# Expert weights of a mixture-of-experts layer loaded in runs of 16384 bytes: seven slots of two megabytes, gate and up over all 2048 columns in four banks each

## The chip, the cores and the metric

The kernel runs on one core of one Trainium2 chip. The metric is the device time in microseconds (us) of one execution. The kernel before takes 2652.8 us, the median of three runs (2651.86 to 2654.31).

## The reference, cut to what matters

The program computes two transformer blocks in float32 on 512 tokens of width 1024. The change lies in the last layer alone: 16 experts, each of which takes the 64 tokens that score highest for it.

```
affinity = softmax(h @ w_router + b_router)
gates, idx = top_k(affinity.transpose(0, 2, 1), 64)          # 64 tokens for each of 16 experts
xin = h[idx]
hid = silu(xin @ w_gate[e]) * (xin @ w_up[e])                # w_gate, w_up: 16 x 1024 x 2048
y   = (hid @ w_down[e]) * gates                              # w_down:       16 x 2048 x 1024
out = x + gate2 * zeros.at[idx].add(y)
```

Each of the three weight arrays of an expert is 8.39 MB (8 binary megabytes); all 16 experts together are 402.65 MB, read once.

## The kernel before, in words

The program is written by hand for five engines: SyncE (SP) issues almost all loads, TensorE (PE) multiplies, ScalarE (ACT) and VectorE (DVE) empty the banks of PSUM. Each engine has its own list of instructions in a fixed order and waits on semaphores of the others. Nothing reorders them at run time.

The experts are worked in eight pairs, n = 0 to 7. The two experts of a pair, d = 0 and 1, lie side by side: the 64 tokens of expert d take columns 64d to 64d+63 of the stationary operand and rows 64d to 64d+63 of a bank. For each n the order on PE is (`pe_experts`, L1205 to L1211):

1. `pe_up` (L1121): gate and up. The 2048 hidden columns are taken in two halves of 1024; in a half, gate over eight k, then up over eight k, in two banks of 512 columns each. The transposes of the first half's hidden values (`pe_moe_turn`, 0 and 1) stand between gate and up of the second half.
2. `pe_scatter` of pair n-1 (L1159): eight products that put the last pair's result back to its tokens; DVE adds each of them to the sum (L2396).
3. `pe_gather` of pair n+1 (L1100): the next pair's tokens are picked by products with a 0/1 matrix (L149), which DVE builds in `dve_gather` just before, and are transposed (L587).
4. `pe_down` (L1143): down over 16 k, two banks; the second half's transposes (`pe_moe_turn`, 2 and 3) stand behind k = 3.

The scatter of the last pair ends the program, and then the result is written.

The weights go through a ring of slots (`Ring`, L104): `Ring.load` waits until PE has signalled that it has used the slot's former load, issues the DMA, and the products wait for its landing. In the expert stage the ring has 13 slots of 1 binary megabyte (8192 bytes on each of the 128 partitions): four in RING, four in RB, two each in AT4 and XT, and one in HID3. One load of gate or up is two blocks k of 128 rows and 1024 columns of one expert, and partition p gets row 128k + p: pieces of 4096 bytes, 8192 bytes apart in memory from one partition to the next. One load of down is two consecutive rows for each partition, 8192 bytes in one piece, 32768 bytes apart. PE signals after every two k, and so sets free the two slots (d = 0 and 1) of one step. `sp_experts` (L409) issues the loads in the order of use; SP does nothing else in this stage.

The trace names tiles by a stage's letter: RB_a is RB, AT_g is AT4, HID_e is HID3, CAT_e is the tokens. An fp32 product stands as two records in the trace.

Of the kernel before, what the change touches and what calls it, by code (L numbers as in the profile page):

```python
# [11 lines left out]
NSLOT = 8  # L12
# [144 lines left out]
def build_program(nc, A, K, out):  # L157
    with ExitStack() as ctx:
# [3 lines left out]
        def sem(name):  # L162
            return ctx.enter_context(nc.semaphore(name))
# [8 lines left out]
        XT = sb("XT", [128, 8, 512])  # L172
# [176 lines left out]
        hidden = TMP[:, 0:2, :].rearrange("p a b -> p (a b)")  # L349
# [3 lines left out]
        PTm = [HID3[:, 12288 + 512 * i:12800 + 512 * i] for i in range(2)]  # L353
        xtok = HID3[:, 13312:14336]
# [54 lines left out]
        def sp_experts(sp, w):  # L409
            for n in range(8):  # L410
                for half in range(2):
                    for m, nm in enumerate(("w_gate_2", "w_up_2")):
                        for kp in range(4):
                            for d in range(2):
                                ring.load(sp, w, ("gu", n, half, m, kp, d),
                                          rows_of(A[nm][0, 2 * n + d], 2 * kp, 1024 * half, 2, 1024), (2, 1024),
                                          (T_moe, "gu", n, half, m, kp))
                for kp in range(8):
                    for d in range(2):
                        rows8 = A["w_down_2"][0, 2 * n + d].rearrange("(h p k) n -> h p k n", h=2, k=8)  # L420
                        ring.load(sp, w, ("dn", n, kp, d), rows8[kp // 4, :, 2 * (kp % 4):2 * (kp % 4) + 2, :],
                                  (2, 1024), (T_moe, "dn", n, kp))

        def sync_program(sp):
# [35 lines left out]
            ring.many, ring.i = NSLOT + 5, 0  # L460
            for i in range(4, 8):
                ring.freed[i] = ((T_out, "out2", 1, 3),)
            for i in range(2):
                ring.freed[NSLOT + i] = ((S_moe, "h2", 3, 1), (T_moe, "router"))
                ring.freed[NSLOT + 2 + i] = ((S_moe, "acc", 3, 1),)
            ring.freed[NSLOT + 4] = ((T_moe, "pos"),)
# [649 lines left out]
        def pe_moe_turn(pe, w, n, fg):  # L1116
            b = banks.take(w, ("hid", n, fg), (S_moe, "hid", n, fg))
            w.wait_ge(*V_moe.at("act", n, fg | 1))
            transposes(pe, b, [hidden[:, 4 * (fg % 2) + j::8] for j in range(4)]).then_inc(*T_moe.up("hid", n, fg))

        def pe_up(pe, w, n):  # L1121
            xv_ = xins[n % 2]
            w.wait_ge(*V_moe.at("xt", n, 0))
            w.wait_ge(*S_moe.at("xt", n, 1))
            for half in range(2):
                fgs = (2 * half, 2 * half + 1)
                for m in range(2):
                    bs = [banks.take(w, ("up" if m else "gate", n, fg), *(((V_moe, "act", n, fg),) if m else
                                                                         ((S_moe, "silu", n, fg),))) for fg in fgs]
                    for k in range(8):  # L1130
                        for c, b in enumerate(bs):
                            for d in range(2):
                                w.wait_ge(*ring.landed("gu", n, half, m, k // 2, d))
                                wv = ring.view("gu", n, half, m, k // 2, d)[:, k % 2, 512 * c:512 * (c + 1)]
                                last = pe.matmul(b[64 * d:64 * d + 64, :], xv_[:, k, 64 * d:64 * d + 64], wv,  # L1135
                                                 start=k == 0, stop=k == 7)
                        if k % 2:
                            last.then_inc(*T_moe.up("gu", n, half, m, k // 2))
                    if half and m == 0:
                        pe_moe_turn(pe, w, n, 0)  # L1140
                        pe_moe_turn(pe, w, n, 1)

        def pe_down(pe, w, n):  # L1143
            bs = [banks.take(w, ("down", n, hf), (V_moe, "y", n, hf)) for hf in range(2)]
            for k in range(16):
                w.wait_ge(*S_moe.at("hid", n, k // 4))
                for hf, b in enumerate(bs):
                    for d in range(2):
                        w.wait_ge(*ring.landed("dn", n, k // 2, d))
                        wv = ring.view("dn", n, k // 2, d)[:, k % 2, 512 * hf:512 * (hf + 1)]  # L1150
                        last = pe.matmul(b[64 * d:64 * d + 64, :], hidT[:, k, 64 * d:64 * d + 64], wv,  # L1151
                                         start=k == 0, stop=k == 15)
                if k % 2:
# [511 lines left out]
        def act_gather(act, w, n):  # L1665
            x = n % 2
            w.wait_ge(*T_moe.at("x", n, 1))
            if n:
                w.wait_ge(*T_moe.at("xt", n - 1, 1))
            act.activation(xtok[:, 512:1024], banks.of("x", n, 1), ACT.Copy, bias=0.0, scale=1.0).then_inc(  # L1670
                *S_moe.up("x", n, 1))
            w.wait_ge(*T_moe.at("pt", n))
            if n >= 2:
                w.wait_ge(*T_moe.at("sc", n - 2, 3, 1))
            act.activation(PTm[x], banks.of("pt", n), ACT.Copy, bias=0.0, scale=1.0).then_inc(*S_moe.up("pt", n))
            w.wait_ge(*T_moe.at("xt", n, 1))
            if n >= 2:
                w.wait_ge(*T_moe.at("gu", n - 2, 1, 1, 3))
            act.activation(xins[x][:, 4:8, :], banks.of("xt", n, 1).rearrange("p (k n) -> p k n", n=128), ACT.Copy,
                           bias=0.0, scale=1.0).then_inc(*S_moe.up("xt", n, 1))  # L1680

        def act_moe_hidden(act, w, n, fg):
            w.wait_ge(*T_moe.at("hid", n, fg))
            if n:
                w.wait_ge(*T_moe.at("dn", n - 1, 7))
# [3 lines left out]
        def act_experts(act, w):  # L1689
# [22 lines left out]
            for n in range(8):  # L1712
                for fg in range(4):
                    q = act_tmp.seat(w, fg % 2, ("hid", n, fg), (T_moe, "hid", n, fg | 1))
                    w.wait_ge(*T_moe.at("gu", n, fg // 2, 0, 3))
                    if fg > 1:
                        act_moe_hidden(act, w, n, fg - 2)
# [4 lines left out]
                act_moe_hidden(act, w, n, 2)  # L1722
                act_moe_hidden(act, w, n, 3)
# [645 lines left out]
        def dve_gather(dve, w, n):  # L2369
# [3 lines left out]
            for i in range(4):  # L2373
                for d in range(2):
# [4 lines left out]
                                      ALU.mult).then_inc(*V_moe.up("P", n, i, d))  # L2379
            w.wait_ge(*T_moe.at("x", n, 0))  # L2380
# [4 lines left out]
            if n >= 2:  # L2385
                w.wait_ge(*T_moe.at("gu", n - 2, 1, 1, 3))
# [11 lines left out]
        def dve_experts(dve, w):  # L2398
# [32 lines left out]
            w.wait_ge(*V_moe.at("pos"))  # L2431
            dve_gather(dve, w, 0)
            for n in range(8):
                for fg in range(4):
                    q = act_tmp.of("hid", n, fg)
                    w.wait_ge(*S_moe.at("silu", n, fg))
                    w.wait_ge(*T_moe.at("gu", n, fg // 2, 1, 3))
# [6 lines left out]
                w.wait_ge(*T_moe.at("dn", n, 7))  # L2444
# [37 lines left out]
        for t in (banks, act_tmp, dve_tmp, lg_tmp, pads, PTs, ring):  # L2482
            t.restart()
# [116 lines left out]
```

## Time and profile before

| | |
|---|---|
| median of 3 runs | 2652.8 us |
| the profiled execution | 2654.73 us |
| its span | 2652.9 us |
| PE busy | 2366.4 us (89%) |
| DVE busy | 1031.9 us (39%) |
| ACT busy | 621.8 us (23%) |
| DMA, mean over the span | 224 GB/s |
| mean granted TensorE clock | 0.958 of 2.4 GHz |

The span is the profiled execution from its first to its last instruction. A share of a busy engine is an average over stages with different limits: the expert stage is the last 40% of the span, and the rows below are mostly from it. DMA share is the mean busy share of the core's 16 DMA engines; packets that overlap make it a little more than 1.

### The profile page before, as it was taken

What the parts mean: (1) busy time and instruction counts of PE and PEld (TensorE: products, weight loads), DVE (VectorE), ACT (ScalarE), POOL (GpSimd) and SP (SyncE); (2) the same over time, 40 slices, a digit from 0 to 9 for tenths busy, and PEclk for the clock granted to TensorE, in tenths of its full rate; (3) what the DMA queues carried; (4) which work ended last, traced back from release to release, by engine and by line L of the source; (5) the groups of instructions that cost most, each with busy time, mean ns of one, the idle gap of its engine ahead of it and who ended that gap; (6) DMA issues with size and microseconds to landing.
All of it is one profiled execution on the core that took longest, in us unless ns stands there. A gap on an engine that the chain in (4) does not pass through costs nothing.

```text
span 2652.9 us, 23645 instructions
## 1 busy us (share of the span) xinstructions
PE 2366.4 (89%) x9809; PEld 1390.5 (52%) x9809; DVE 1031.9 (39%) x1633; ACT 621.8 (23%) x1000; POOL 129.2 (5%) x133
## 2 busy tenths in 40 slices
PE   5999988899999599999789888887989797988888
PEld 2446444688887288888667647332323233332323
DVE  4565462566654866564656353110101101010102
ACT  2112162323322333223446454000000000000000
POOL 2000000000000200000321322000000000000000
PEclk8999988999999699999889998899999999999999
DMA  8312410255552145550211203799999999999998
GB/s 344 103 64 87 147 68 25 104 191 183 179 190 88 55 149 184 190 190 18 93 56 32 76 29 128 301 423 419 397 421 401 421 400 422 398 409 413 407 418 333
DMA packets 181440, 594.21 MB, mean 224 GB/s; under 512 B 12418, under 2 KB 13952, under 8 KB 163798
## 3 DMA queue, kind: packets, MB, share of 16 engines
q1 hardware_dynamic: 177938, 583.24, 57.1%
q0 software_dynamic: 3088, 9.33, 1.0%
q8 instruction: 77, 1.26, 0.2%
q14 instruction: 29, 0.24, 0.0%
q10 hardware_dynamic: 308, 0.13, 0.0%
HBM read 590.54 MB, written 2.13 MB: 223 GB/s over the span
## 4 chain that ended last, share of the span: by engine, by line
PE 69%; DMA 18%; DVE 8%; ACT 3%; issue 1%; SPq 1%; POOL 0%; ACTq 0%; DVEq 0%; POOLq 0%
PE PS L863 9%; PE PS L865 9%; PE PS L864 9%; PE PS L679 7%; PE PS L1151 7%; PE PS L889 5%; PE PS L149 5%; PE PS L1135 5%; DMA RING<-in_w_up_dram 3%; DMA RB_a<-in_w_up_dram 3%; PE PS L1165 2%; DMA RING<-in_w_gate_dram 2%; DMA XT<-in_w_up_dram 2%; PE PS L587 2%; PE PS L763 2%; DMA XT<-in_w_gate_dram 1%
## 5 line engine op out<-in xcount | busy, mean ns | idle before, releaser
L2438 DVE TENSOR_TENSOR TMP<-TMP,PS 128x512 f32<-128x512 f32 x32 | 20.6, 684 | 559.1 <-PE PS L1135 559.1
L1135 PE MATMUL PS<-RING,HID_e 128*64 128x512 f32 x656 | 186.3, 597 | 33.5 <-DMA RING<-in_w_up_dram 18.9
L1135 PE MATMUL PS<-RB_a,HID_e 128*64 128x512 f32 x624 | 178.2, 597 | 27.9 <-DMA RB_a<-in_w_up_dram 16.5
L1135 PEld LDWEIGHTS PS<-RING,HID_e 128*64 128x64 f32 x656 | 57.9, 136 | 133.1 <-issue 69.4
L1135 PE MATMUL PS<-XT,HID_e 128*64 128x512 f32 x320 | 110.2, 597 | 15.6 <-DMA XT<-in_w_up_dram 8.6
L1135 PEld LDWEIGHTS PS<-RB_a,HID_e 128*64 128x64 f32 x624 | 56.9, 137 | 118.1 <-issue 62.7
L1135 PE MATMUL PS<-AT_g,HID_e 128*64 128x512 f32 x296 | 102.4, 597 | 13.0 <-DMA AT_g<-in_w_up_dram 7.7
L1686 ACT ACTIVATE HID_e<-PS 128x512 f32<-128x512 f32 x32 | 18.3, 598 | 386.2 <-PE PS L587 386.2
L863 PE MATMUL PS<-AH_b,WH_b 128*128 128x512 f32 x256 | 101.8, 398 | 3.2 <-DVE AL_b L1805 3.2
L863 PE MATMUL PS<-AH_d,WH_d 128*128 128x512 f32 x256 | 101.8, 398 | 3.2 <-DVE AL_d L1805 3.2
L865 PE MATMUL PS<-AH_b,WL_b 128*128 128x512 f32 x256 | 100.6, 393 | 0.0
L865 PE MATMUL PS<-AH_d,WL_d 128*128 128x512 f32 x256 | 100.6, 393 | 0.0
L864 PE MATMUL PS<-AL_b,WH_b 128*128 128x512 f32 x256 | 100.5, 393 | 0.0
L864 PE MATMUL PS<-AL_d,WH_d 128*128 128x512 f32 x256 | 100.5, 393 | 0.0
L2448 DVE TENSOR_TENSOR HID_e<-PS,HID_e 128x512 f32<-128x512 f32 x16 | 10.3, 686 | 231.9 <-PE PS L1151 231.9
L863 PE MATMUL PS<-HH_d,WH_d 128*128 128x512 f32 x256 | 100.4, 392 | 0.0
L863 PE MATMUL PS<-HH_b,WH_b 128*128 128x512 f32 x256 | 100.4, 392 | 0.0
L865 PE MATMUL PS<-HH_b,WL_b 128*128 128x512 f32 x256 | 99.9, 390 | 0.0
L865 PE MATMUL PS<-HH_d,WL_d 128*128 128x512 f32 x256 | 99.9, 390 | 0.0
L864 PE MATMUL PS<-HL_b,WH_b 128*128 128x512 f32 x256 | 99.7, 390 | 0.0
L864 PE MATMUL PS<-HL_d,WH_d 128*128 128x512 f32 x256 | 99.7, 390 | 0.0
L149 PE MATMUL PS<-CAT_e,HID_e 128*128 128x512 f32 x128 | 71.2, 721 | 31.3 <-DVE HID_e L2378 31.3
(447 smaller groups left out, 4591.6 us busy)
## 6 DMA issues: line engine op xcount, KB each, us to landing
RB_a<-in_w_gate_dram SPq DMA_DIRECT2D x42, 1024.0 KB, 16.6
RING<-in_w_gate_dram SPq DMA_DIRECT2D x41, 1024.0 KB, 17.8
RING<-in_w_up_dram SPq DMA_DIRECT2D x41, 1024.0 KB, 18.1
RB_a<-in_w_down_dram SPq DMA_DIRECT2D x41, 1024.0 KB, 21.1
RING<-in_w_down_dram SPq DMA_DIRECT2D x38, 1024.0 KB, 23.6
RB_a<-in_w_up_dram SPq DMA_DIRECT2D x36, 1024.0 KB, 18.0
RING<-in_mlp_w_dram SPq DMA_DIRECT2D x32, 1024.0 KB, 5.7
RB_a<-in_mlp_w_dram SPq DMA_DIRECT2D x32, 1024.0 KB, 5.4
```

What stands on the lines that cost most here:

```text
L149: last = pe.matmul(out, l, r, start=i == 0, stop=i == len(pairs) - 1)
L587: last = pe.transpose(out[0:n, 128 * i:128 * i + x.shape[0]], x, ident[0:x.shape[0], 0:x.shape[0]])
L679: last = pe.matmul(b, ring.view(name, *label, k // 4)[:, k % 4, j * 128:(j + 1) * 128], rhs(k), start=k == 0, stop=k == 7)
L763: last = pe.matmul(b, lhs, ring.view("v", k // 4)[:, k % 4, :], start=False, stop=k == 7)
L863: pe.matmul(b, hi[:, kk, js], a[:, k, :], start=k == 0, stop=False)
L864: pe.matmul(b, hi[:, kk, js], al[:, k, :], start=False, stop=False)
L865: last = pe.matmul(b, lo[:, kk, js], a[:, k, :], start=False, stop=k == 7)
L889: last = pe.matmul(b, x, y, start=k == 0 and i == 0, stop=k == 7 and i == 2)
L1135: last = pe.matmul(b[64 * d:64 * d + 64, :], xv_[:, k, 64 * d:64 * d + 64], wv, start=k == 0, stop=k == 7)
L1151: last = pe.matmul(b[64 * d:64 * d + 64, :], hidT[:, k, 64 * d:64 * d + 64], wv, start=k == 0, stop=k == 15)
L1165: pe.matmul(b, PTm[n % 2][:, i * 128:(i + 1) * 128], yB[:, hf * 512:(hf + 1) * 512], start=True, stop=True).then_inc(*T_moe.up("sc", n, i, ...
L2438: dve.tensor_tensor(q, q, banks.of("up", n, fg), ALU.mult).then_inc(*V_moe.up("act", n, fg))
```

## The change

The ring of 13 slots of 1 binary megabyte in the expert stage becomes a ring `big` of seven slots of 2: RING in two, RB in two, AT4, XT, and HID3 from column 12288 (it was one slot from 14336). Two small buffers, `xtok` and `PTm`, move out of HID3 into PADS for that.

Gate and up are loaded so that partition p gets eight consecutive rows, 8p to 8p+7, over all 2048 columns; one load is two of them, 16384 bytes in one piece, 65536 bytes apart from one partition to the next. One load of down is four consecutive rows, 16384 bytes, 32768 bytes apart. There are 24 loads for a pair in place of 48. The tokens are transposed with a stride of 8 columns to match.

PE goes over gate in four banks, all eight k, and then over up in four banks. All four transposes of hidden values stand at the head of `pe_down`. A gate or up step now uses two loads of 2 binary megabytes and signals after two k; a step of down signals after four k in place of two. The hidden values take four TMP buffers in place of two. On DVE the building of the 0/1 matrices for pair n+1 (`dve_chosen`) moves from behind the scatter of n-1 to ahead of the products of gate and up of n. The first transpose of the gathered tokens now waits for both halves of `xtok`, where each waited for its own.

```diff
-        hidden = TMP[:, 0:2, :].rearrange("p a b -> p (a b)")
+        hid_tmp = Turns([TMP[:, i, :] for i in range(4)])
+        hidden = TMP[:, 0:4, :].rearrange("p a b -> p (a b)")
+        loose = PADS[:, :, :].rearrange("p a b -> p (a b)")
...
-        for i, ap in enumerate([AT4[:, 0:4, :], AT4[:, 4:8, :], XT[:, 0:4, :], XT[:, 4:8, :]]):
-            ring.add(ap.rearrange("p a b -> p (a b)"), sem(f"ring{NSLOT + i}"))
-        ring.add(HID3[:, 14336:16384], sem(f"ring{NSLOT + 4}"))
+        big = Ring()
+        for i, ap in enumerate([RING[:, 0:2, :], RING[:, 2:4, :], RB[:, 0:2, :], RB[:, 2:4, :], AT4[:, :, :], XT[:, :, :]]):
+            big.add(ap.rearrange("p a b -> p (a b)"), sem(f"big{i}"))
+        big.add(HID3[:, 12288:16384], sem("big6"))
...
         def sp_experts(sp, w):
             for n in range(8):
-                for half in range(2):
-                    for m, nm in enumerate(("w_gate_2", "w_up_2")):
-                        for kp in range(4):
-                            for d in range(2):
-                                ring.load(sp, w, ("gu", n, half, m, kp, d),
-                                          rows_of(A[nm][0, 2 * n + d], 2 * kp, 1024 * half, 2, 1024), (2, 1024),
-                                          (T_moe, "gu", n, half, m, kp))
-                for kp in range(8):
+                for m in range(2):
+                    for kp in range(4):
+                        for d in range(2):
+                            rows8 = A[("w_gate_2", "w_up_2")[m]][0, 2 * n + d].rearrange("(p k) n -> p k n", k=8)
+                            big.load(sp, w, ("gu", n, m, kp, d), rows8[:, 2 * kp:2 * kp + 2, :], (2, 2048),
+                                     (T_moe, "gu", n, m, kp))
+                for kq in range(4):
                     for d in range(2):
                         rows8 = A["w_down_2"][0, 2 * n + d].rearrange("(h p k) n -> h p k n", h=2, k=8)
-                        ring.load(sp, w, ("dn", n, kp, d), rows8[kp // 4, :, 2 * (kp % 4):2 * (kp % 4) + 2, :],
-                                  (2, 1024), (T_moe, "dn", n, kp))
+                        big.load(sp, w, ("dn", n, kq, d), rows8[kq // 2, :, 4 * (kq % 2):4 * (kq % 2) + 4, :], (4, 1024),
+                                 (T_moe, "dn", n, kq))
...
-                w.wait_ge(*(S_moe if hf else V_moe).at("x", n, hf))
-                transposes(pe, b, [xtok[:, (4 * hf + k) * 128:(4 * hf + k + 1) * 128] for k in range(4)]).then_inc(
+                w.wait_ge(*V_moe.at("x", n, 0))
+                w.wait_ge(*S_moe.at("x", n, 1))
+                transposes(pe, b, [xtok[:, 4 * hf + k::8] for k in range(4)]).then_inc(
...
         def pe_down(pe, w, n):
+            for t in range(4):
+                pe_moe_turn(pe, w, n, t)
             bs = [banks.take(w, ("down", n, hf), (V_moe, "y", n, hf)) for hf in range(2)]
...
-                if k % 2:
-                    last.then_inc(*T_moe.up("dn", n, k // 2))
-                if k == 3:
-                    pe_moe_turn(pe, w, n, 2)
-                    pe_moe_turn(pe, w, n, 3)
+                if k % 4 == 3:
+                    last.then_inc(*T_moe.up("dn", n, k // 4))
...
             for n in range(8):
+                if n < 7:
+                    dve_chosen(dve, w, n + 1)
                 for fg in range(4):
-                    q = act_tmp.of("hid", n, fg)
+                    q = hid_tmp.of("hid", n, fg)
```

## Rows read from the trace of the kernel before

**Rows 1.** The page: the span, what DMA moved in 40 equal slices, and packets.

```profile
span 2652.9 us, 23645 instructions
GB/s 344 103 64 87 147 68 25 104 191 183 179 190 88 55 149 184 190 190 18 93 56 32 76 29 128 301 423 419 397 421 401 421 400 422 398 409 413 407 418 333
DMA packets 181440, 594.21 MB, mean 224 GB/s; under 512 B 12418, under 2 KB 13952, under 8 KB 163798
```

**Rows 2.** Windows, stretches of one pair: length, engines' busy time, PEclk, DMA share, GB/s.

```profile
1885.00:1892.00 7.00, 7.00 (x38) 2.81 (x37) 0.69 (x1) 1.41 (x3) 0.00 (x0) 1.00 0.63 236
1900.00:1907.00 7.00, 7.00 (x35) 2.31 (x33) 0.00 (x0) 0.00 (x0) 0.00 (x0) 1.00 1.01 369
1907.00:1983.00 76.00, 64.31 (x288) 22.26 (x284) 2.58 (x4) 3.15 (x6) 0.00 (x0) 1.00 1.03 419
```

**Rows 3.** Windows: down alone (first, last of six pairs), gate and up alone (likewise).

```profile
1865.00:1885.00 20.00, 16.14 (x37) 6.99 (x38) 10.46 (x27) 0.28 (x1) 0.00 (x0) 0.91 1.01 428
2479.00:2499.00 20.00, 16.13 (x38) 6.98 (x38) 10.40 (x27) 0.38 (x1) 0.00 (x0) 0.91 1.01 426
...
1930.00:1982.00 52.00, 40.66 (x180) 14.56 (x178) 1.29 (x2) 2.07 (x4) 0.00 (x0) 1.00 1.03 421
2544.00:2596.00 52.00, 40.31 (x179) 14.02 (x176) 1.29 (x2) 2.06 (x4) 0.00 (x0) 1.00 1.03 419
```

**Rows 4.** The chain that ended last, one turnover: start us, us, what.

```profile
1843.05 18.19 DMA RING<-in_w_up_dram
...
1861.28 3.65 PE PS L1135 x14
1864.93 7.08 PE PS L1165 x16
...
1875.86 8.83 PE PS L149 x16
1884.69 1.34 PE PS L587 x12
1886.03 7.02 PE PS L1151 x32
1893.05 1.09 PE PS L587 x8
```

**Rows 5.** Windows of 1 us in the dip; the last two columns are DMA share and GB/s.

```profile
1885.00:1886.00 1.00, 1.00 (x12) 0.78 (x9) 0.40 (x1) 0.81 (x2) 0.00 (x0) 1.00 0.89 377
...
1887.00:1888.00 1.00, 1.00 (x8) 0.30 (x6) 0.00 (x0) 0.00 (x0) 0.00 (x0) 1.00 0.50 213
...
1890.00:1891.00 1.00, 1.00 (x8) 0.31 (x6) 0.00 (x0) 0.00 (x0) 0.00 (x0) 1.00 0.87 197
```

**Rows 6.** Timeline of SP's DMA issues, two turnover rows and the first after the start.

```profile
1864.97 25.49 SPq L132 DMA_DIRECT2D RING<-in_w_down_dram  x4
1893.09 0.33 SPq L132 DMA_DIRECT2D RB_a<-in_w_down_dram  x1
...
1685.26 3.80 SPq L132 DMA_DIRECT2D RING<-in_w_up_dram  x3
```

**Rows 7.** Timeline of PE: start, us, what, and in brackets the idle time before.

```profile
1861.28 3.65 PE L1135 MATMUL PS<-RING,HID_e 128*64 128x512 f32 x14 [1.43 <-DMA RING<-in_w_up_dram]
...
1875.86 8.83 PE L149 MATMUL PS<-CAT_e,HID_e 128*128 128x512 f32 x16 [3.86 <-DVE HID_e L2378]
...
488.83 1.02 PE L628 MATMUL PS<-ones,TMP 128*128 128x1 f32 x8 [2.98 <-DVE MODC L1769]
```

**Rows 8.** Windows behind those idle times: the third number from the end is the granted clock.

```profile
1876.00:1880.00 4.00, 4.00 (x6) 1.69 (x7) 0.00 (x0) 0.00 (x0) 0.00 (x0) 0.57 1.01 428
1880.00:1884.00 4.00, 4.00 (x10) 1.72 (x9) 0.69 (x1) 0.00 (x0) 0.00 (x0) 1.00 1.01 426
...
490.50:496.00 5.50, 2.29 (x9) 2.02 (x10) 2.41 (x4) 2.68 (x4) 0.00 (x0) 0.50 1.05 400
```

**Rows 9.** Windows at the start of the stage, DMA's last two columns.

```profile
1672.00:1685.00 13.00, 12.27 (x42) 5.58 (x43) 1.38 (x2) 2.97 (x4) 0.00 (x0) 0.89 0.02 6
```

**Rows 10.** The chain that ended last, the last pair.

```profile
2602.12 7.06 PE PS L1165 x16
...
2637.62 3.66 PE PS L1151 x14
```

More of the change, by code:

```diff
@@ L352, in build_program @@
         Pg = [HID3[:, 11264 + 512 * i:11776 + 512 * i].rearrange("p (t n) -> p t n", t=4) for i in range(2)]
[L353 to L357 removed]
+        PTm = [loose[:, 1024 + 512 * i:1536 + 512 * i] for i in range(2)]
+        xtok = loose[:, 0:1024]
+        big = Ring()
+        for i, ap in enumerate([RING[:, 0:2, :], RING[:, 2:4, :], RB[:, 0:2, :], RB[:, 2:4, :], AT4[:, :, :], XT[:, :, :]]):
+            big.add(ap.rearrange("p a b -> p (a b)"), sem(f"big{i}"))
+        big.add(HID3[:, 12288:16384], sem("big6"))
         parts = [(T_ml, "xm"), (T_ml, "so"), (T_ml, "av"), (T_dil, "ak"), (T_dil, "aq"), (T_out, "out2", 0),
@@ L459, in sync_program @@
                     ring.load(sp, w, (*parts[b][1:], kh), rows_of(W, 4 * kh, c0), (4, 512), (G_prt, b, 4 * kh + 3))
[L460 to L466, printed above, removed]
+            big.many = 7
+            big.freed[0] = (*ring.freed[0], *ring.freed[1])
+            big.freed[1] = (*ring.freed[2], *ring.freed[3])
+            big.freed[2] = big.freed[3] = ((T_out, "out2", 1, 3),)
+            big.freed[4] = ((S_moe, "h2", 3, 1), (T_moe, "router"))
+            big.freed[5] = ((S_moe, "acc", 3, 1),)
+            big.freed[6] = ((T_moe, "pos"),)
             sp_experts(sp, w)
@@ L1111, in pe_gather, with pe_moe_turn @@
                 b = banks.take(w, ("xt", n, hf), (S_moe if hf else V_moe, "xt", n, hf))
-                w.wait_ge(*(S_moe if hf else V_moe).at("x", n, hf))
-                transposes(pe, b, [xtok[:, (4 * hf + k) * 128:(4 * hf + k + 1) * 128] for k in range(4)]).then_inc(
+                w.wait_ge(*V_moe.at("x", n, 0))
+                w.wait_ge(*S_moe.at("x", n, 1))
+                transposes(pe, b, [xtok[:, 4 * hf + k::8] for k in range(4)]).then_inc(
                     *T_moe.up("xt", n, hf))
[L1116 to L1119, printed above, removed]
+        def pe_moe_turn(pe, w, n, t):
+            b = banks.take(w, ("hid", n, t), (S_moe, "hid", n, t))
+            w.wait_ge(*V_moe.at("act", n, t | 1))
+            o = 1024 * (t // 2) + 4 * (t % 2)
+            transposes(pe, b, [hidden[:, o + j:1024 * (t // 2 + 1):8] for j in range(4)]).then_inc(*T_moe.up("hid", n, t))
         def pe_up(pe, w, n):
@@ L1124, in pe_up @@
             w.wait_ge(*S_moe.at("xt", n, 1))
[L1125 to L1136, printed above, removed]
-                        if k % 2:
[L1138 to L1141, printed above, removed]
+            for m in range(2):
+                bs = [banks.take(w, ("up", n, fg), (V_moe, "act", n, fg)) if m else
+                      banks.take(w, ("gate", n, fg), (S_moe, "silu", n, fg)) for fg in range(4)]
+                for k in range(8):
+                    for c, b in enumerate(bs):
+                        for d in range(2):
+                            w.wait_ge(*big.landed("gu", n, m, k // 2, d))
+                            wv = big.view("gu", n, m, k // 2, d)[:, k % 2, 512 * c:512 * (c + 1)]
+                            last = pe.matmul(b[64 * d:64 * d + 64, :], xv_[:, k, 64 * d:64 * d + 64], wv,
+                                             start=k == 0, stop=k == 7)
+                    if k % 2:
+                        last.then_inc(*T_moe.up("gu", n, m, k // 2))
         def pe_down(pe, w, n):
+            for t in range(4):
+                pe_moe_turn(pe, w, n, t)
             bs = [banks.take(w, ("down", n, hf), (V_moe, "y", n, hf)) for hf in range(2)]
@@ L1148, in pe_down @@
                     for d in range(2):
-                        w.wait_ge(*ring.landed("dn", n, k // 2, d))
-                        wv = ring.view("dn", n, k // 2, d)[:, k % 2, 512 * hf:512 * (hf + 1)]
+                        w.wait_ge(*big.landed("dn", n, k // 4, d))
+                        wv = big.view("dn", n, k // 4, d)[:, k % 4, 512 * hf:512 * (hf + 1)]
                         last = pe.matmul(b[64 * d:64 * d + 64, :], hidT[:, k, 64 * d:64 * d + 64], wv,
                                          start=k == 0, stop=k == 15)
-                if k % 2:
-                    last.then_inc(*T_moe.up("dn", n, k // 2))
-                if k == 3:
-                    pe_moe_turn(pe, w, n, 2)
-                    pe_moe_turn(pe, w, n, 3)
+                if k % 4 == 3:
+                    last.then_inc(*T_moe.up("dn", n, k // 4))
         def pe_scatter(pe, w, n):
@@ L1721, in act_experts @@
                     act_gather(act, w, n + 1)
-                act_moe_hidden(act, w, n, 2)
-                act_moe_hidden(act, w, n, 3)
+                for t in range(4):
+                    act_moe_hidden(act, w, n, t)
         def scalar_program(act):
@@ L2379, in dve_gather @@
                                       ALU.mult).then_inc(*V_moe.up("P", n, i, d))
+        def dve_gather(dve, w, n):
+            x = n % 2
             w.wait_ge(*T_moe.at("x", n, 0))
@@ L2481, in build_program @@
             s.restart()
-        for t in (banks, act_tmp, dve_tmp, lg_tmp, pads, PTs, ring):
+        for t in (banks, act_tmp, dve_tmp, lg_tmp, hid_tmp, pads, PTs, ring, big):
             t.restart()
```

19 lines of the change are left out of this document (9 added, 10 removed).

## The prediction

> **What bounds the kernel now.** I read the page's slices first. DMA moves about 400 to 420 GB/s from slice 27 to 39 [rows 1]: the expert stage streams its 402.65 MB near one constant rate, so I then took one pair of experts apart. From the scatter at 1864.93 to the last pair's at 2602.12 there are six pairs in 737.2 us, 122.87 us each [rows 4, 10]. In that time 50.33 MB must come. Windows over stretches with one kind of load give the rates: gate and up, in 4096-byte packets, 421 to 419 GB/s, down, in 8192-byte packets, 428 to 426, with DMA share 1.01 to 1.03 in both [rows 3]. So 33.55 MB / 0.420 = 79.9 us and 16.78 / 0.4265 = 39.3 us. Two flaws are left. In 1885 to 1892 the rate is 236, which loses 7 x (1 - 236/426.5) = 3.1 us; in 1900 to 1907 it is 369 at full share, which loses 0.85 us [rows 2]. Sum 123.2 us, 0.3 more than the measured period. The DMA engines are the bound, and the dip is the only time in which they lack work.
>
> The dip's cause stands in the chain and the timeline of SP. Call T the landing of a pair's last up load (1861.28) and E the end of its products (1864.93). From E on PE scatters (7.08 us), waits 3.86 us for DVE, gathers (8.83), transposes (1.34), and only the first two k of down (half of the 7.02 us for four) set slots free: 1889.5, T + 28.25 [rows 4, 7]. SP's row of four loads that starts at 1864.97 ends at 1890.46: two went out at E, two after that release [rows 6]. Meanwhile the 13 slots hold 13.63 MB, 32.0 us of transfer at 426.5. At 1887 the share is exactly 0.50 with 213 GB/s [rows 5]: half of the DMA engines have drained, the others are some 4 us behind, and work resumes around 1890.5.
>
> **The change part by part.**
>
> *Packet size.* A 4096-byte packet on one of 16 engines takes 4096 x 16 / 420 GB/s = 156.0 ns, one of 8192 bytes 307.3 ns [rows 3]. The line through both is 4.7 ns plus 151.3 ns for 4096 bytes; an estimate for 16384 bytes from it is 609.9 ns, 430 GB/s. No such packet of a load is in the trace. Bounds: the 8192-byte rate of 426.5 from below if larger packets bring nothing more, 433 from above with no cost per packet (8192 x 16 / 302.6); rows for a worse end are weighed as a rival. I take 430, since share and rate speak for engines that are bound by themselves. Per pair: gate and up 78.0 us (-1.9), down 39.0 (-0.3): -2.2 us.
>
> The Trainium skill (DMA: Bandwidth & Descriptors, section Why small descriptors are slow (HBM only)) says that each packet costs about three cycles of the engine's internal bus beside its beats of 32 bytes. An estimate by that page would be 515 cycles for 16384 bytes, 433 GB/s with its 850 MHz, and a pair 0.7 us shorter than in my sum; the trace's 4.7 ns lies above its 3.5.
>
> *Fewer issues.* 24 loads in place of 48. SP's issues wait for room or for slots and are never what the chain waits for at the turnover except through the slot; gain 0, bounds 0 and 0.33 us (one issue [rows 6]) per turnover.
>
> *Coarser steps at T.* A step of gate or up was 16 records in two 1 MB loads and is 32 in two 2 MB loads. Of the old step 14 records ran after the last landing, 3.65 us [rows 4]; of the new one 30, that is 3.65 + 3.45 = 7.1 us. E comes 3.45 us later against T, each pair.
>
> *The chain from E to the first release.* Scatter 7.08 as before; DVE has four products to do at E where it had two, but PE's fifth scatter needs their banks only after 3.5 us, four times 0.69. The wait of 3.86 us goes, since the 0/1 matrices are built during gate; with it goes the low clock behind it: granted 0.57 in the next 4 us, 1.00 after [rows 8], that is between the 1.2 and 2.4 GHz levels, so the gather at full clock takes 16 x 0.43 = 6.9 us, not 8.83. The transposes of tokens now wait for ACT's copy of the second half, some 0.5 us, and take a strided operand as those of the hidden values do, 1.09 / 8 = 0.136 us against 1.34 / 12 = 0.112 [rows 4]: 2.0 us in place of 1.34. All four hidden transposes stand ahead of down: 16 x 0.136 = 2.2 us. The first release comes after four k, 7.02 us. Sum 7.08 + 6.9 + 2.0 + 2.2 + 7.0 = 25.2 us, against 24.6 before. ACT's three copies and the first hidden copy, 0.6 us each, end inside PE's transposes. With the coarser step the release moves from T + 28.25 to T + 32.3: +4.05.
>
> *The ring's depth.* Seven slots hold 14.68 MB, 34.1 us at 430: +2.1 against 32.0. So the dip grows by 4.05 - 2.1 = 1.9 us, from 3.1 to 5.0. What waits behind this release on SP is the whole next stream, and through it PE.
>
> *Clock in gate and up.* PE now works 6.9 us and idles about 2.7 of every 9.75, where it idled 1.43 of 5 at granted clock 1.00 [rows 2, 7]. An idle time of 2.98 us was followed by 0.50 [rows 7, 8]. A fall during the last step of a pair makes E up to 1.7 us later (as much as the gather loses now: 8.83 - 6.9 = 1.9). Elsewhere DMA hides it: 6.9 + 1.9 < 9.75. Bounds 0 and 1.9; I take 0.5, nearer to the rows with 1.00.
>
> *A pair with a dip:* -2.2 + 1.9 + 0.5 = +0.2 us, six times: +1.2.
> *Pair 0 to 1:* no scatter, so release at T + 25.2 and no dip; -2.2.
> *The start:* DMA stands still from 1672 with all slots full until PE's first release near 1685.2 [rows 6, 9]. That release comes 3.45 us (coarser step) and 0.6 us (transposes) later, but 1.05 MB more has landed: of pair 0's gate and up 18.87 MB are left at 430 (43.9 us) in place of 19.92 at 420 (47.4): +0.55.
> *The end:* the last down is bound by its landings; transfer -0.3, and 30 records follow the last landing in place of 14: +3.45 - 0.3 = +3.15 [rows 10].
> The moves of buffers, the order of banks, the four TMP buffers: 0, as each is freed by work many microseconds back; bounds 0 and 0.6 (one ACT copy) per pair.
>
> Sum: 1.2 - 2.2 + 0.55 + 3.15 = +2.7 us, on the profiled execution's 2654.73 us (span 2652.9 [rows 1]). That execution lies 1.9 us above the median of the runs, and the forecast is made on the median: 2655.5.
>
> **Rivals.**
>
> *The dip doesn't grow (faster).* If the two halves of the DMA engines drain together, or the chain is shorter than summed, the gain of the packets is kept: 7 x -2.2 + 0.55 + 3.15 = -11.7, 2641; with the dip gone as well (-3.1 x 6) 2622. For it: the lag of half the engines is what opens the dip early [rows 5], and the slow stretch of 369 GB/s [rows 2] may be where it arises; both may change. Against: the release itself comes 4 us later.
>
> *The turnover decides (slower).* Place: PE between T and the first release of down. With the low clock in the last step (+1.9 in place of 0.5) and no gain beyond the 8192-byte rate (-1.2 for gate and up), a pair is -1.2 + 1.9 + 1.9 = +2.6: 6 x 2.6 - 1.2 + 0.8 + 3.4 = +18.6, 2671. It decides from the point where dip and clock together grow by more than the 2.2 us that packets give. For it: the rows on 2.98 us of idle time; against: 1.43 us never cost anything.
>
> *The change doesn't do what it says.* Packets might be cut to 8192 bytes: then only gate and up gain 1.2 us, a pair with a dip is +1.2, and the sum 7.2 - 1.2 + 0.8 + 3.4 = +10, 2663. For it: no load in the trace has larger ones; against: the packets below 8 KB leave 17642 others [rows 1], as many as down's 16384 pieces need, so pieces go out whole so far.
>
> *Distance in memory.* Gate and up come from addresses 65536 bytes apart per partition, where it was 8192. If that made every gate and up load as slow as the stretch of 369 GB/s, 33.55 MB would take 90.9 us, +11 a pair and some +90 in all; a tenth of that is +9, 2662. Against: down at 32768 is the faster one [rows 3].
> The Trainium skill (DMA: Bandwidth & Descriptors, Latency and other measured facts, HBM row pitch) reports loss at row pitches of large powers of two, small at 512 KiB (207 GB/s against 214) and large from 2 MiB; by it 64 KiB would cost at most those 3%, which no run here shows.
>
> **How the numbers follow.** Forecast 0.38; dip no larger 0.25; turnover decides 0.20; packets cut 0.10; distance 0.07. A difference under 0.2% (5.3 us) can't be told from none here. The forecast case is mostly within it (0.30 same, 0.05 slower, 0.03 faster), the second faster (0.23, 0.02 same), the third slower (0.17, 0.03 same), the fourth too (0.09, 0.01), the fifth slower (0.07): faster 0.26, same 0.36, slower 0.38. The forecast's own range is 2648 to 2662; with the rivals' ends 2636 to 2673.
>
> **What would show it.** Rate over gate and up near 430 in place of 420, and half as many DMA issues, show the packets. The dip should last about 2 us longer and begin about 2 us later after T; no idle time of PE ahead of the gather and a gather of 6.9 us show the moved DVE work; idle times of 2.7 us with granted clock 1.00 or not show the clock. At the end 30 records follow the last landing. Wrong would be: a period under 120 us (dip not grown), a rate at or under 420 (packets or distance), or a chain from E to the first release far from 25 us.

## The result and the profile after

The changed kernel takes 2626.56 us (median of 4 runs, 2625.84 to 2627.95) against 2653.14 us for the kernel before beside it: ratio 0.9901, 95% interval 0.9883 to 0.9918. That is 26.6 us faster; the forecast was 2.3 us slower, with a range down to 2636. It was wrong.

The page after, with the lines that answer to [rows 1] (the last one is the queue of SP's loads):

```profile
span 2626.1 us, 23460 instructions
GB/s 348 104 65 80 136 89 4 109 192 192 192 189 84 64 144 179 190 186 39 88 49 33 92 29 129 212 431 431 424 430 410 430 422 431 412 416 426 415 430 326
DMA packets 121024, 594.19 MB, mean 226 GB/s; under 512 B 9346, under 2 KB 10881, under 8 KB 95191
q1 hardware_dynamic: 117522, 583.23, 56.1%
```

The slices of the expert stage rise from about 400 to 420 to 410 to 431, and 60,416 packets fewer move the same bytes, so the loads did go out in larger pieces. (By size, 402.65 MB in pieces of 16384 bytes need 24,576 packets, and 81,920 in pieces of 4096 and 8192: 57,344 fewer. The other 3,072 are packets under 512 bytes, 16 for each of the 192 loads that are gone.)

The windows of the changed kernel over down alone (first and last of six pairs) and over gate and up alone, which answer to [rows 3]; the last three columns are the granted clock, DMA share and GB/s:

```profile
1859.00:1879.00 20.00, 19.66 (x71) 10.03 (x72) 8.84 (x14) 3.64 (x7) 0.00 (x0) 1.00 1.01 431
2458.00:2478.00 20.00, 19.66 (x74) 9.92 (x74) 8.37 (x14) 3.64 (x7) 0.00 (x0) 1.00 1.01 429
...
1922.00:1974.00 52.00, 39.69 (x168) 12.23 (x166) 0.00 (x0) 2.06 (x4) 0.00 (x0) 0.93 1.01 430
2530.00:2582.00 52.00, 43.12 (x170) 14.01 (x167) 4.99 (x9) 2.06 (x4) 0.00 (x0) 0.93 1.01 431
```

Both kinds now run at 429 to 431, where the line through the two rates of before gave 430. The granted clock is 0.93 in the gate and up windows, where it was 1.00.

The chain of waits of the changed kernel over one turnover, the last step of two more and the end, which answers to [rows 4, 10]:

```profile
1852.18 7.08 PE PS L1137 x30
1859.26 7.07 PE PS L1163 x16
1866.33 6.88 PE PS L149 x16
1873.97 2.90 PE PS L589 x24
1876.88 27.62 PE PS L1152 x128
...
2208.84 8.78 PE PS L1137 x30
...
2568.43 8.47 PE PS L1137 x30
...
2607.43 7.09 PE PS L1152 x30
```

Each step is there as it was summed: 30 records behind the landing in 7.08 us, no wait ahead of the gather, a gather of 6.88 us, and the transposes, which with the wait ahead of them take 3.7 us from the gather's end to down where 4.2 were forecast. In the other two turnovers the last step takes 8.78 and 8.47 us. Over the six turnovers behind pairs 1 to 6 it took 7.08 us twice and 8.5 to 8.8 us four times. There the clock was low. The idle time of PE ahead of such a step, and the granted clock right behind another landing at 1970.93, near the lower of its two levels:

```profile
1852.18 0.64 PE L1137 MATMUL PS<-AT_g,HID_e 128*64 128x512 f32 x1 [2.60 <-DMA AT_g<-in_w_up_dram]
...
1970.50:1974.00 3.50, 3.07 (x8) 1.00 (x10) 0.00 (x0) 0.00 (x0) 0.00 (x0) 0.51 1.01 431
```

SP's issues in the changed kernel in the turnovers that follow 1852.18 and 2208.84; a row's start is the moment of release when SP waited:

```profile
1859.66 0.43 SPq L132 DMA_DIRECT2D AT_g<-in_w_down_dram  x1
1883.93 0.33 SPq L132 DMA_DIRECT2D XT<-in_w_down_dram  x1
...
2218.02 0.43 SPq L132 DMA_DIRECT2D HID_e<-in_w_down_dram  x1
2242.32 0.33 SPq L132 DMA_DIRECT2D RING<-in_w_down_dram  x1
```

Counted from the landing T of the pair's last up load, the first release comes at T + 31.75 (1883.93 - 1852.18) and T + 33.5; the forecast was T + 32.3 and up to 1.9 more. The dip, in windows of the changed kernel: first after the turnover at 1859 (1 row), then 1 us each after the one at 1979, then two of the length that answers to [rows 2] (1900 to 1907 and the rest of the pair):

```profile
1884.00:1886.00 2.00, 2.00 (x12) 0.71 (x10) 0.00 (x0) 0.00 (x0) 0.00 (x0) 1.00 0.83 246
...
2002.00:2003.00 1.00, 1.00 (x6) 0.29 (x4) 0.00 (x0) 0.00 (x0) 0.00 (x0) 1.00 0.35 148
2003.00:2004.00 1.00, 1.00 (x8) 0.34 (x6) 0.00 (x0) 0.00 (x0) 0.00 (x0) 1.00 0.15 66
2004.00:2005.00 1.00, 1.00 (x8) 0.38 (x6) 0.00 (x0) 0.00 (x0) 0.00 (x0) 1.00 0.00 0
2005.00:2006.00 1.00, 1.00 (x6) 0.29 (x4) 0.00 (x0) 0.00 (x0) 0.00 (x0) 1.00 1.15 262
...
1900.00:1907.00 7.00, 7.00 (x36) 2.40 (x34) 2.46 (x9) 0.00 (x0) 0.00 (x0) 1.00 1.02 435
1907.00:1972.00 65.00, 50.28 (x220) 16.07 (x218) 1.91 (x10) 2.06 (x4) 0.00 (x0) 0.96 1.01 430
```

In the kernel before, the row of share 0.50 in [rows 5] stood between two more like it:

```profile
1886.00:1887.00 1.00, 1.00 (x7) 0.43 (x8) 0.29 (x1) 0.60 (x1) 0.00 (x0) 1.00 0.56 238
...
1888.00:1889.00 1.00, 1.00 (x6) 0.29 (x4) 0.00 (x0) 0.00 (x0) 0.00 (x0) 1.00 0.54 229
```

The changed kernel has no such plateau of some 3 us: the engines work at full rate to T + 31 or T + 32 and fall silent nearly together, within 2 us, and the stretch of 369 GB/s [rows 2] is gone (435). From landing to landing a pair takes (2568.43 - 1852.18) / 6 = 119.4 us, before 122.87.

Where the 26.8 us between the two spans lie, by the landings T in the two chains (those of before at 1742.05, 1861.28 and 2598.47; after at 1735.35, 1852.18 and 2568.43): up to pair 0's landing -6.7, of which 1.3 lies ahead of the expert stage; pair 0 to 1 -2.4; the six pairs -20.9; the end +3.2. The stage's first gather, by which I take its start, begins anywhere from 1665.4 to 1671.1 us in the profiled executions of all runs, so a few us of a difference between two spans can lie ahead of anything that was changed. Below, pairs are therefore mostly compared from landing to landing.

### The profile page after: what moved, and what is told of

Read it like the earlier page. It is cut to its first block, busy times and chain, and to the rows that moved or that the text cites. A ratio compares the mean times of both kernels' runs of the same rounds, so it can differ in the third digit from the quotient of the medians.

```text
span 2626.1 us, 23460 instructions
## 1 busy us (share of the span) xinstructions
PE 2361.5 (90%) x9809; PEld 1384.4 (53%) x9809; DVE 1028.1 (39%) x1633; ACT 620.2 (24%) x1000; POOL 129.2 (5%) x133
## 4 chain that ended last, share of the span: by engine, by line
PE 73%; DMA 15%; DVE 7%; ACT 3%; issue 1%; POOL 0%; ACTq 0%; DVEq 0%; POOLq 0%
PE PS L865 9%; PE PS L1137 9%; PE PS L867 9%; PE PS L866 9%; PE PS L681 7%; PE PS L1152 7%; PE PS L891 5%; PE PS L149 5%; DMA RING<-in_w_up_dram 4%; DMA RB_a<-in_w_up_dram 3%; PE PS L1163 2%; PE PS L589 2%; DMA HID_e<-in_w_up_dram 2%; PE PS L765 2%; DMA XT<-in_w_up_dram 2%; DMA AT_g<-in_w_up_dram 2%
## 5 line engine op out<-in xcount | busy, mean ns | idle before, releaser
L1137 PE MATMUL PS<-RING,HID_e 128*64 128x512 f32 x608 | 214.6, 628 | 28.9 <-DMA RING<-in_w_up_dram 20.7
L1137 PE MATMUL PS<-RB_a,HID_e 128*64 128x512 f32 x576 | 202.3, 614 | 28.7 <-DMA RB_a<-in_w_up_dram 21.7
L1137 PE MATMUL PS<-XT,HID_e 128*64 128x512 f32 x288 | 138.5, 633 | 15.7 <-DMA XT<-in_w_up_dram 10.6
L1137 PE MATMUL PS<-HID_e 128*64 128x512 f32 x288 | 136.7, 627 | 17.7 <-DMA HID_e<-in_w_up_dram 11.4
L1137 PE MATMUL PS<-AT_g,HID_e 128*64 128x512 f32 x288 | 136.5, 627 | 11.6 <-DMA AT_g<-in_w_up_dram 7.3
L1137 PEld LDWEIGHTS PS<-RING,HID_e 128*64 128x64 f32 x608 | 64.9, 145 | 125.9 <-issue 83.6
L1714 ACT ACTIVATE TMP<-PS 128x512 f32<-128x512 f32 x32 | 16.5, 603 | 456.9 <-PE PS L1137 456.9
L1137 PEld LDWEIGHTS PS<-RB_a,HID_e 128*64 128x64 f32 x576 | 63.1, 141 | 109.7 <-issue 67.4
```

## The experiments

Every run is compared with the kernel before on the same chip; that one had medians of 2651.5 to 2653.8. "Against the change" is against the 2626.56 us above.

**e1: small packets from the new addresses.** Based on the changed kernel.

Loads of down stay as they are; the issues of gate and up double.

```diff
+    def load_halves(self, sp, w, label, src, *freed):
...
+        view = self.aps[b].rearrange("p (h k c) -> p h k c", h=2, k=2)
+        for h in range(2):
+            sp.dma_start(view[:, h], src[:, :, 1024 * h:1024 * (h + 1)]).then_inc(self.sems[b], 16)
+        self.n[b] += 32
...
-                            big.load(sp, w, ("gu", n, m, kp, d), rows8[:, 2 * kp:2 * kp + 2, :], (2, 2048),
-                                     (T_moe, "gu", n, m, kp))
+                            big.load_halves(sp, w, ("gu", n, m, kp, d), rows8[:, 2 * kp:2 * kp + 2, :],
+                                            (T_moe, "gu", n, m, kp))
```

> The changed kernel, with each gate and up load of two binary megabytes issued as two DMAs of 1024 columns each: packets of 4096 bytes from the same addresses, the same slots and the same steps. Theory A (the lag of half the DMA engines before came from addresses 8192 bytes apart between partitions): no lag, the dip as in the changed kernel, and only the packets' price, 33.55 MB at 420 in place of 431 GB/s = +2.0 us a pair, 7.7 pairs' worth = +16: about 2642 us. Rival B (the lag comes from small packets as such, wherever they come from): the lag and the long dip return as well, +2 to +3 us at each of six turnovers on top: 2655 to 2660 us.

Measured 2642.35 us, ratio 0.9960 (0.9945 to 0.9974). As theory A has it: +15.8 against the change, which is the packets' price alone.

**e2: larger packets from the old addresses.**

```diff
-                            big.load(sp, w, ("gu", n, m, kp, d), rows8[:, 2 * kp:2 * kp + 2, :], (2, 2048),
+                            big.load(sp, w, ("gu", n, m, kp, d),
+                                     rows_of(A[("w_gate_2", "w_up_2")[m]][0, 2 * n + d], 2 * kp, 0, 2, 2048), (2, 2048),
...
```

> The changed kernel, with gate and up loaded as rows 128k + p over all 2048 columns: pieces of 8192 bytes, 8192 bytes apart between partitions, the same slots and steps. Theory A (addresses): the slow stretch after each turnover and the lag of half the engines return, +3 us at six turnovers, beside +1.0 us a pair for packets of 8192 bytes (8 us in all): about 2652 us. Rival B (packet size): only the packets' price and perhaps a little lag: 2634 to 2638 us.

Measured 2631.82 us, ratio 0.9914 (0.9898 to 0.9931). Theory A fails here: rows 8192 bytes apart bring no lag back as long as whole rows are loaded. It is also 2 us below the range of rival B; against the change the packets of 8192 bytes cost 5.3 us where 8 were expected.

**e3: the kernel before with eight rows per partition.**

```diff
-                                          rows_of(A[nm][0, 2 * n + d], 2 * kp, 1024 * half, 2, 1024), (2, 1024),
+                                          A[nm][0, 2 * n + d].rearrange("(p k) n -> p k n", k=8)[
+                                              :, 2 * kp:2 * kp + 2, 1024 * half:1024 * (half + 1)], (2, 1024),
...
```

> The kernel before, with gate and up loaded as eight consecutive rows for each partition (4096-byte pieces, 65536 bytes apart between partitions), tokens transposed to match; 13 slots of one binary megabyte as before. Theory A (addresses): slow stretch and lag go; the slots drain at T + 30 where the release comes at T + 28.3, so the dip of 3.1 us and the slow stretch of 0.85 go six times: -20 to -24, about 2631 us. Rival B (packet size): nothing changes, 2653 us within 3.

Measured 2637.37 us, ratio 0.9937 (0.9923 to 0.9952): -16.5 with packets, slots and steps as before. Rival B fails here. Theory A has the direction right but expected 20 to 24: a pair takes 120.8 us from landing to landing ((2579.37 - 1854.66) / 6), 2.1 less than before and still some 1.8 more than 50.33 MB at its rates. Windows of e3 over its dip and over the stretch that had 369 GB/s, and one of e2 and one of e1 over that stretch:

```profile
1884.00:1888.00 4.00, 4.00 (x23) 1.69 (x19) 0.00 (x0) 0.34 (x1) 0.00 (x0) 1.00 0.92 342
1900.00:1907.00 7.00, 7.00 (x36) 2.37 (x34) 0.00 (x0) 0.00 (x0) 0.00 (x0) 1.00 1.03 421
```

```profile
1900.00:1907.00 7.00, 7.00 (x34) 2.30 (x32) 0.00 (x0) 0.00 (x0) 0.00 (x0) 1.00 1.01 427
```

```profile
1900.00:1907.00 7.00, 7.00 (x34) 2.30 (x32) 0.00 (x0) 0.00 (x0) 0.00 (x0) 1.00 1.02 417
```

In e3 the microseconds of the dip have shares of 0.76, 0.89 and 0.71 (1883 to 1886), so half of the engines no longer run dry 3 us ahead. Neither small packets (e1, e3) nor rows 8192 bytes apart (e2) make the slow stretch or the lag by themselves. It comes with their combination in the kernel before: half a row from each of 128 neighbouring rows. That combination was not tried with the slots and steps of the changed kernel.

The start of the stage says the same. From the first gather to pair 0's landing, across the standstill with full slots, it takes 72.2 us in the kernel before and 71.6 in e4 below, which both have the old loads, and 66.8 in the change, 68.1 in e1, 67.3 in e2 and 67.5 in e3.

**e4: the kernel before with the matrices built early.** This is the DVE part of the change alone.

```diff
             for n in range(8):
+                if n < 7:
+                    dve_chosen(dve, w, n + 1)
                 for fg in range(4):
...
```

> The kernel before, with the 0/1 matrices of pair n+1 built on DVE ahead of the products of pair n, as the change does; nothing else. PE's wait of 3.86 us and the low clock in the gather go, so the first release of down comes 5.8 us earlier, at T + 22.5, before even the first half of the DMA engines has drained (T + 24.6). If all engines bind alike, the whole dip goes: 6 x -3.1 = -18.6, about 2634 us. If the lagging half binds alone (it stood idle only some 1.2 us of each turnover), only that is gained: 6 x -1.2 = -7, about 2646 us. If DMA did not bind at all there, more than -19.

Measured 2631.3 us, ratio 0.9917 (0.9902 to 0.9932): -22.4. The chain of e4: its first turnover and its last landing, then the first gather of the stage in e4 and, last, in the kernel before:

```profile
1856.57 3.65 PE PS L1135 x14
1860.22 7.06 PE PS L1165 x16
1867.29 6.87 PE PS L149 x16
...
1875.50 7.02 PE PS L1151 x32
...
2574.80 3.65 PE PS L1135 x14
...
1665.73 9.60 PE PS L149 x16
...
1669.84 9.59 PE PS L149 x16
```

The wait ahead of the gather and the low clock in it are gone, and the first two k of down end at T + 22.4. Of the 23.0 us between the two spans, 19.0 lie in the six turnovers, 3.2 each, as "the whole dip goes" has it. Another 4.1 lie ahead of the stage, where nothing was changed. A pair takes 119.7 us, 0.5 over the 119.2 of its two rates. Windows of e4 over what were the dip and the slow stretch, and one over its start, behind the standstill with full slots:

```profile
1884.00:1891.00 7.00, 7.00 (x36) 2.42 (x34) 0.00 (x0) 0.28 (x1) 0.00 (x0) 1.00 1.00 422
1891.00:1898.00 7.00, 7.00 (x36) 2.32 (x34) 0.00 (x0) 0.00 (x0) 0.00 (x0) 1.00 1.02 420
...
1695.00:1700.00 5.00, 5.00 (x26) 2.06 (x24) 0.00 (x0) 0.00 (x0) 0.00 (x0) 1.00 1.01 364
```

At the turnover dip and slow stretch are both gone, with the old addresses and packets still in place; at the start, where the standstill stays, so does the slow stretch. So the slow stretch is something that follows a standstill. All engines bind alike. This one part is most of the gain: all the rest of the change adds some 4.7 us to it (2626.56 against 2631.3), and the two intervals overlap.

**e5: the changed kernel with the matrices late again.** The two lines of e4's diff move back behind `dve_scatter`.

> The changed kernel, with the building of the 0/1 matrices put back behind the scatter. PE waits for DVE again (3.9 us) and gathers at the low clock (+1.9), so the first release of down comes 5.8 us later. Theory (DMA engines bind, and stand idle from about T + 32 until that release): the idle time grows by all of it at six turnovers: +35, about 2661 us. If part of the wait lies in slack of PE and the slots still cover it: +10 to +20.

Measured 2664.19 us, ratio 1.0039 (1.0024 to 1.0054): +37.6 against the change. By landings, 31.8 of the 37.3 us between the spans lie in the six turnovers, 5.3 each of the 5.8 expected, and 4.7 between pair 0 and 1, which had no dip in the change. It is 10.4 us slower than the kernel before (2653.84 beside it): without the early matrices, the new loads, slots and steps are a loss. With the wait back, the windows of e5 have 7 us (1889 to 1896) at DMA share 0.12.

```profile
1889.00:1896.00 7.00, 7.00 (x35) 2.30 (x33) 0.00 (x0) 0.13 (x1) 0.00 (x0) 1.00 0.12 49
```

**e6: six slots.**

```diff
-            big.many = 7
+            big.many = 6
```

> The changed kernel with six of its seven slots. 2.1 MB less in flight is 4.9 us of transfer, so the engines drain at T + 27 in place of T + 32: +4.9 us at six turnovers, and +4.9 at the start, where one load less has landed: +34, about 2661 us. If the idle time measured at the turnover were no idle time of the bound (something else ended last there): under +10.

Measured 2657.68 us, ratio 1.0017 (1.0007 to 1.0026): +31.1. By landings a turnover costs 4.0 us more and the start 4.9 more (the profiled execution was the fastest of ten). In the first turnover the engines stand nearly still from 1881 on:

```profile
1881.00:1887.00 6.00, 6.00 (x32) 2.00 (x30) 0.00 (x0) 0.00 (x0) 0.00 (x0) 1.00 0.10 41
```

So the turnover has its price from the side of the supply too, by what the slots hold.

**e7: the same memory in 14 small slots.**

```diff
-                            big.load(sp, w, ("gu", n, m, kp, d), rows8[:, 2 * kp:2 * kp + 2, :], (2, 2048),
-                                     (T_moe, "gu", n, m, kp))
+                            big.load(sp, w, ("gu", n, m, kp, d), rows8[:, kp, :], (2048,), (T_moe, "gu", n, m, kp))
...
-                    if k % 2:
-                        last.then_inc(*T_moe.up("gu", n, m, k // 2))
+                    last.then_inc(*T_moe.up("gu", n, m, k))
...
-            big.many = 7
+            big.many = 14
```

> The changed kernel with the same 14 binary megabytes cut into 14 slots of one: a load of gate or up is one row of 2048 columns per partition, one of down two rows, all in packets of 8192 bytes, and PE signals after each k of gate and up and after two k of down. E comes 3.45 us earlier after T and the first release another 3.5: at about T + 25, before the engines drain, so no dip. A pair is then 50.33 MB at 426.5 GB/s = 118.0 us against 119.6: six times -1.6, pair 0 +1.1, start -3.0, end -3.0: about 2612 us. If packets of 16384 bytes matter more than the steps, slower than 2626.

Measured 2619.59 us, ratio 0.9868 (0.9853 to 0.9883). Faster than the change, by 7 in place of the 14 expected; the two intervals just meet at 0.9883, and that of e10 below, the change once more, overlaps with it by 0.0008. The pairs are right to a half: from scatter to scatter (2567.34 - 1856.17) / 6 = 118.5 us, expected 118.0. The missing 7 lie in two places: the six pairs gain 5.1 us against the change and not 9.6, and the stage begins 2.5 us later (first gather at 1671.07 against 1668.55). Start and end are as expected (-1.9 expected up to pair 1's landing, -2.2 measured within the stage; -3.0 at the end, measured -3.3). So smaller packets with finer steps beat larger ones with coarser steps, by 5 to 7 us.

**e8: the gather behind down.**

```diff
-                if n < 7:
-                    pe_gather(pe, w, n + 1)
                 pe_down(pe, w, n)
+                if n < 7:
+                    pe_gather(pe, w, n + 1)
```

And the same in ACT's and DVE's lists.

> The changed kernel with the gather of pair n+1 behind the products of down, on PE, ACT and DVE, slots and loads as in the change. The first release comes about 8 us earlier, near T + 24, before the engines drain at T + 32: no dip, 50.33 MB at 431 = 116.8 us a pair against 119.6: -2.8 at six turnovers, -17, about 2610 us. If the gather's copies, now right ahead of the next gate products, hold PE back by more than its slack, the gain is smaller.

Measured 2616.22 us, ratio 0.9859 (0.9843 to 0.9876): 10 us under the change, where 17 were expected. Windows of e8 over the whole of a pair, turnover included, and two rows of its chain, the scatters of pairs 1 and 7:

```profile
1857.00:1909.00 52.00, 49.51 (x204) 19.69 (x202) 13.06 (x32) 3.75 (x7) 0.00 (x0) 1.00 1.01 431
1909.00:1974.00 65.00, 57.24 (x245) 19.13 (x242) 0.15 (x1) 2.06 (x4) 0.00 (x0) 0.95 1.01 431
```

```profile
1857.87 7.06 PE PS L1163 x16
...
2564.00 7.06 PE PS L1163 x16
```

No dip is left, here or in the five pairs that follow (430 or 431 throughout), and a pair takes 117.7 us, 0.9 over 50.33 MB at 431.

**e9 and e10: a shorter end, beside the change itself.** In e9 the last load of down of each expert of pair 7 is two loads of one binary megabyte.

```diff
-                for kq in range(4):
+                for kq in range(3 if n == 7 else 4):
...
+            for h in range(2):
+                for d in range(2):
+                    rows8 = A["w_down_2"][0, 14 + d].rearrange("(h p k) n -> h p k n", h=2, k=8)
+                    big.load(sp, w, ("dn", 7, 3 + h, d), rows8[1, :, 4 + 2 * h:6 + 2 * h, :], (2, 1024), (T_moe, "dn", 7, 3))
```

> The gather behind down, and beside it the last load of down of each expert of pair 7 in two loads of one binary megabyte, so that 14 records follow the last landing in place of 30: -3.45 us at the end, nothing elsewhere, about 2612.5 us where the gather behind down alone gave 2616.2. If the end is bound by DVE and the scatter and not by the last products, no change.

> The changed kernel itself, unchanged, beside the last one on the same chip: 2626 to 2628 us by every theory; it is here so that the two are compared in the same rounds.

e9 measured 2615.19 us, ratio 0.9858 (0.9843 to 0.9873); e10 2625.12, ratio 0.9892 (0.9875 to 0.9910). The short end is a miss: no gain over e8's ratio of 0.9859. The end was no longer bound by its loads in e8 either, whose last down also runs through (128 records in 28.35 us from 2572.81), so there was nothing to shorten. The chain of e9:

```profile
2565.08 7.06 PE PS L1169 x16
2572.15 1.79 PE PS L593 x16
2573.94 27.64 PE PS L1158 x128
```

All 128 records of the last down run without a wait for a load, and the end is bound by PE. What the runs bear out as best is e8 or e9, 1.4% faster than the kernel before and some 10 us faster than the change.

## Why the prediction was wrong

**What bounds the kernel: right.** The DMA engines bind: less supply (e6) and a later release (e5) cost 31 and 38 us with the same loads and the same products.

**Packet size: right.** -2.2 us a pair forecast at 430 GB/s; 429 to 431 measured. The one turnover without a dip, pair 0 to 1, gave -2.4. The estimate of 433 GB/s from the Trainium skill (DMA: Bandwidth & Descriptors, Why small descriptors are slow (HBM only)) is high by 2 to 4. e1, with 4096-byte packets back, costs +15.8, that is 2.05 for each of the 7.7 pairs' worth that were expected to pay.

**Coarser steps and the chain: right.** The last products end at T + 7.08 against 7.1 (where the clock was not low), the first release comes 24.7 us after that against 25.2.

**The ring's depth: this is the step that failed.** I wrote that the seven slots add only 2.1 us of supply, "So the dip grows by 4.05 - 2.1 = 1.9 us, from 3.1 to 5.0". That took over from the kernel before the moment at which its first half of the engines drained and moved it by the difference in bytes. Measured, the dip after is one of 2 us at 246 GB/s in the first turnover and about 3 in later ones. A pair's 119.4 us less 50.33 MB at 431 (116.8) leaves 2.6 us of loss, low clock included, where the forecast had 5.0 and 0.5; before, dip and slow stretch together took 3.65 (122.87 less 119.2). The sign that I had named for being wrong, a period under 120 us, is what came. The engines now work to T + 32. The seven slots hold 34.1 us of transfer; that the landing at T lags some 2 behind its transfer would explain the difference, but no run shows it. Before, half of them stopped at T + 24.6 of a supply of 32.0 us.

That lag of half the engines was no constant of the ring. It belonged to half-row loads from neighbouring rows: with other addresses alone and the old slots, packets and steps, it is gone (e3: 421 in place of 369, and no plateau of 0.50). In e4 the release comes ahead of T + 24.6, so whether the lag is still there can't be seen. I had named the lag as what spoke for the rival "the dip doesn't grow". The measured time lies between that rival's 2641 and its further end of 2622, with the dip gone as well; I gave it 0.25 in all, and left the range at 2636, above an end of my own rival.

**The slow stretch: left out of the sum.** I counted its 0.85 us as a flaw of before, but gave it no term in the sum, so that the forecast kept it in every pair. It vanished in the changed kernel (435 where it was 369). Dip and slow stretch together account for the 3.7 us by which a pair missed the forecast (123.1 against 119.4), and six times that for 22 of the 29.5 us in all.

**The start: wrong by 6.** +0.55 forecast, -5.4 measured (pair 0's landing at 1735.35 against 1742.05, less the 1.3 us by which the stage began earlier). The same cause once more, behind the standstill with full slots: new addresses alone give -4.7 (e3), early matrices alone -0.6 (e4). Windows of the kernel before and then of the changed one, from about the first release on:

```profile
1685.00:1689.00 4.00, 4.00 (x22) 1.66 (x20) 0.00 (x0) 0.00 (x0) 0.00 (x0) 1.00 0.61 201
1689.00:1695.00 6.00, 6.00 (x32) 2.42 (x30) 0.00 (x0) 0.00 (x0) 0.00 (x0) 1.00 1.01 394
1695.00:1705.00 10.00, 10.00 (x50) 4.05 (x48) 0.00 (x0) 1.09 (x2) 0.00 (x0) 1.00 1.02 354
```

```profile
1688.00:1692.00 4.00, 4.00 (x21) 1.58 (x19) 0.00 (x0) 0.00 (x0) 0.00 (x0) 1.00 0.81 274
1692.00:1705.00 13.00, 13.00 (x64) 5.35 (x62) 0.00 (x0) 0.00 (x0) 0.00 (x0) 1.00 1.02 436
```

The old loads run at 354 GB/s for ten microseconds after that standstill too; the new ones are at 436 from four us behind the first release on.

**Clock in gate and up: right in kind, too small.** In four of the six turnovers the last step took 8.5 to 8.8 us in place of 7.08, 1.0 us on average, where 0.5 was taken and 1.9 was the bound. It lies within the 2.6 us of loss. In e10, the same kernel again, it was two of the six, and a pair took 119.0 us.

**The end: right,** +3.15 forecast, +3.2 measured.

**The other rivals.** The turnover did decide, but the other way: e4 and e5 show that the release's time is the strongest lever in either kernel. I had the right price for moving the matrices, 5.8 us earlier; it was set against a dry moment that came too early. Packets were not cut. Addresses 65536 bytes apart cost nothing: 430 GB/s over gate and up. The Trainium skill's loss at large row pitches (DMA: Bandwidth & Descriptors, Latency and other measured facts, HBM row pitch) did not appear at 64 KiB; no run here tried its larger ones.

What stays open: why half of the engines fall behind with that combination of pieces. The runs show when it comes and goes, not by what in the memory. Open too are the 1.8 us of a pair in e3 beyond its rates, and why e8 gained 10 and not 17.

## What to carry to other kernels

Where a stream of loads is the bound, price two moments against each other: when the slots in flight run dry and when the first one is set free again. As long as the release comes behind the dry moment, everything on the chain between them counts nearly in full, also work of an engine that is idle 60% of the time. 5.8 us of it cost 5.3 us a turnover where the release then came too late (e5). They gave 3.2 where the release moved ahead of the dry moment (e4), since there was no more to win. In all that was 38 and 22 us; going back to packets a quarter as large cost 16 (e1). Ask of the dry moment in the old trace whether all engines reach it together; if half of them stop early, that lag is an effect of this kernel's loads and can't be carried into the sum for another layout.

## What the runs showed of the hardware

Packets of 4096, 8192 and 16384 bytes moved at 420, 426.5 and 430 to 431 GB/s on 16 engines, close to one straight line in time (156.0, 307.3 and 608 to 610 ns).

After a standstill, loads of half a row (4096 bytes) from each of 128 neighbouring rows of 8192 bytes ran at 354 to 369 GB/s at full DMA share for 7 to 10 us (kernel before; 364 at the start of e4), and at the next dip half of the engines ran dry some 3 to 4 us ahead of the others. The same packets from rows 65536 bytes apart (e3, 421) and whole neighbouring rows (e2, 427) did not.

Beside idle times of TensorE of 2.6 us between 7 us of work, some stretches had the lower of the two clock levels (granted 0.51 behind the landing at 1970.93, mean 0.93 over gate and up); beside 1.4 us between 3.6 us of work, all six gate and up stretches of the kernel before had 1.00.
